# One layer of a hybrid DeltaNet and sliding-window attention encoder: four edits to the order and width of small steps in a fused kernel

## The chip, the cores and the metric

The kernel runs on one core of a Trainium2 chip. The metric is the device time of the program in microseconds (us); less is better. The core's engines are TensorE (PE in the profile, its weight loads PEld), VectorE (DVE), ScalarE (ACT), GpSimd (POOL) and SyncE (SP, which issues DMAs here). Each works through its own list of instructions in order, and they meet only at semaphores.

## The reference

One layer over 2048 positions of width 1024, in fp32:

```python
h = rms_norm(x, norm_w)
z = h @ w_in     # q,k,v of branch A, b_a, a_a (8 columns each), z_a; q,k,v,z of branch B; gates
qkv = silu(causal_depthwise_conv(concat([qa, ka, va]), conv_w))      # 4 taps
beta = sigmoid(b_a);  g = -exp(a_log) * softplus(a_a + dt_bias)
oa = gated_delta_rule(l2(qa), l2(ka), va, g, beta)                   # chunks of 64
# per chunk and head, n_mat strictly lower triangular, 64 x 64:
#   t_mat = I + n_mat; p = n_mat
#   5 times: p = p @ p;  t_mat = t_mat + t_mat @ p
ya = (rms_norm(oa, gdn_norm_w) * silu(z_a)) @ w_o_a
ob = swa_sink_attention(qb, kb, vb, sinks, bias) * silu(z_b)         # window of 2 chunks
m = sigmoid(gate_a) * ya + sigmoid(gate_b) * (ob @ w_o_b)
out = rms_norm(x + m @ w_out, final_norm_w)
```

There are 8 DeltaNet heads with keys and values of 128, and 16 attention heads of 64 on 2 key heads.

## The kernel before

The sequence is cut into 4 blocks (`b`) of 512 positions, each with 4 chunk pairs (`t`, 128 positions). Every large product is a "gemm" of one weight tile of 1024 x 128 (`USES` lists their order): 8 steps over the contraction, each of three matmuls of 128x512 (L1214, L1215, L1216), since an fp32 factor is split into a high and a low part of type fp32r. A block has 3 tiles of prologue (`pro`: beta and decay padded from 16 to 128 columns, then the attention's keys and values), 48 of heads (6 each), 16 gates, 8 + 8 for the branches' output projections (`ya`, `yb`) and 8 for `out`. In block 0 each tile comes fresh: SP loads it, ACT rounds the high part (`high_part`, L485), POOL subtracts the low part (L408), SP stores both to HBM; later blocks load that copy into one of three slots.

Branch A and B of head `h` run in `head`, while the projections of head `h+1` fill the gaps: on PE, ACT and DVE `project` is a generator, and `fill(n)` runs its next n steps. These counts are written by hand, and they set each engine's order.

On DVE the steps of `project` are, for each of q, k and v: one scaling (L923) and three multiply-adds of the convolution (L927), of which the last increments `conv_ready[i]`, then the product with the tanh (L909); and then L909 for za and zb. On ACT they are, in order: copy q, copy k, tanh of q's convolution, copy v, tanh of k's convolution (L575, which waits for `conv_ready[1]`), the three copies of the attention's q, tanh of v's, and two tanhs more.

In `head`, after the decay matrix and k.kT, DVE writes the strictly lower matrix (L970), POOL having given `rk` (a power, L421) for it. PE transposes it (L1400). Five levels follow on PE, each with `square` (p = p @ p, L1331) and `apply` (p @ [p | t], L1347) for the two halves `g` of the chunks, and a sixth `apply`; ACT and DVE copy the results back between them. Then the state goes through the four chunk pairs: PE k.s (L1421), q.s (L1426), DVE r (L1057), PE y (L1431), ACT copies y (L706), PE the state's increment (L1436), DVE the state (L1063) and o (L1067). On ACT this part is written as

```python
state(2)          # o1 copy (L703), y copy (L706)
fill(1)           # tanh of k's convolution
probs_copy(1)
square_o(1)
fill(1)           # three copies of the attention's q
state(3)
```

At the end POOL takes another power (`rqo`), PE transposes o (L1449), and DVE multiplies it into za (L1095) and splits it into `oa_hi` (L1098) and `oa_lo` (L1099), which increments `head_dve_done`.

## Time and profile before

| | |
|---|---|
| median of 3 runs | 2762.26 us (2761.41 to 2763.84) |
| the profiled execution: its own time | 2763.31 us |
| its span in the trace | 2761.2 us, granted TensorE clock 0.999 |
| PE busy | 2722.1 us, 99% of the span |
| DVE, ACT, POOL busy | 1400.4, 981.4, 408.7 us |
| one head in block 1, PE's L1302 to the next head's | 54.85 us (1042.21 to 1097.04) |

How to read it: a row of the timeline gives the start, the time from the first start to the last end, the engine, line and operation, what is written and read, shapes, and how many instructions are merged in it; in brackets is the engine's idle time before it and what ended that. PE's matmuls overlap in the records (one of 128x512 shows 0.39 us, while the next starts 0.23 us after it), so on PE the distance between starts is what counts. An fp32 matmul shows as two records. A "q" after an engine's name is its sequencer, which issues DMAs.

### The profile page before, as it was taken

The numbers are of one execution on the slowest core, as the hardware profiler recorded it, in microseconds if no ns is written. First come the engines' busy times: TensorE is split into PE (matmuls) and PEld (weight loads), VectorE is DVE, ScalarE is ACT, GpSimd is POOL, SyncE is SP. The second block draws the span as 40 slices with busy tenths as digits, with TensorE's granted clock in tenths as the row PEclk, the third lists the DMA queues.
The fourth block names the chain that finished last, engine by engine and source line by source line (L and its number), as shares of the span: only waits on it lengthen the run. The fifth ranks groups of instructions, "written<-read, shape, count | busy, mean of one in ns | idle before, by whom it ended". The sixth has DMA issues, their size and how long they took to land.

```text
span 2761.2 us, 50479 instructions
## 1 busy us (share of the span) xinstructions
PE 2722.1 (99%) x19888; PEld 2305.2 (83%) x19888; DVE 1400.4 (51%) x3529; ACT 981.4 (36%) x3165; POOL 408.7 (15%) x240
## 2 busy tenths in 40 slices
PE   7999999999999999999999999999999999999998
PEld 6888888888888888888888888888888888888887
DVE  5677777323266666622236666661224666665012
ACT  4554555432244444421114444442112444434101
POOL 4333333343210101000000011000000011000000
PEclk9999999999999999999999999999999999999999
DMA  7554445688643233345563333325555333333564
GB/s 259 188 183 157 169 172 185 228 281 295 253 143 127 99 121 125 125 180 209 190 222 120 110 123 124 116 106 203 210 192 209 123 110 125 123 114 108 184 227 168
DMA packets 79577, 463.08 MB, mean 168 GB/s; under 512 B 13296, under 2 KB 17392, under 8 KB 31856
## 3 DMA queue, kind: packets, MB, share of 16 engines
q1 hardware_dynamic: 65808, 430.47, 43.7%
q10 hardware_dynamic: 13536, 29.40, 3.0%
q8 instruction: 160, 2.62, 0.4%
q14 instruction: 73, 0.60, 0.1%
HBM read 356.02 MB, written 103.81 MB: 167 GB/s over the span
## 4 chain that ended last, share of the span: by engine, by line
PE 93%; DVE 3%; DMA 1%; POOL 1%; issue 1%; ACT 0%; ACTq 0%; DVEq 0%; SPq 0%; POOLq 0%
PE bank L1214 23%; PE bank L1216 23%; PE bank L1215 23%; PE bank L1347 5%; PE bank L1331 3%; PE bank L1314 2%; PE bank L1393 1%; PE bank L1431 1%; PE bank L1302 1%; PE bank L1436 1%; PE bank L1385 1%; PE bank L1378 1%; PE bank L1370 1%; PE bank L1439 1%; PE bank L1426 1%; PE bank L1421 1%
## 5 line engine op out<-in xcount | busy, mean ns | idle before, releaser
L1214 PE MATMUL bank<-hT_hi,w_sl 128*128 128x512 f32 x2144 | 885.9, 413 | 0.7 <-ACT hT_hi L516 0.7
L1216 PE MATMUL bank<-hT_hi,w_sl 128*128 128x512 f32 x2144 | 838.9, 391 | 0.0
L1215 PE MATMUL bank<-hT_lo,w_sl 128*128 128x512 f32 x2144 | 836.7, 390 | 0.0
L1216 PEld LDWEIGHTS bank<-hT_hi,w_sl 128*128 128x128 f32 x2144 | 402.4, 188 | 88.1
L1214 PEld LDWEIGHTS bank<-hT_hi,w_sl 128*128 128x128 f32 x2144 | 403.9, 188 | 72.7 <-ACT hT_hi L516 0.9
L1215 PEld LDWEIGHTS bank<-hT_lo,w_sl 128*128 128x128 f32 x2144 | 404.6, 189 | 66.3 <-issue 0.7
L408 POOL TENSOR_TENSOR w_sl<-w_raw,w_sl 128x1024 fp32r<-128x1024 f32 x91 | 222.0, 2444 | 399.4 <-ACT w_sl L485 399.4
L927 DVE SCALAR_TENSOR_TENSOR area<-zraw,stc,area 128x512 f32<-128x512 f32 x288 | 220.3, 765 | 4.2
L1347 PE MATMUL bank<-area 64*64 64x128 f32 (+1 forms) x3072 | 197.9, 245 | 1.1 <-issue 0.6
L822 DVE TENSOR_SCALAR area<-bank 128x128 f32<-128x128 f32 (+1 forms) x320 | 101.4, 317 | 154.8 <-PE bank L1347 114.5
L1063 DVE SCALAR_TENSOR_TENSOR s_cur<-s_cur,scs,bank 128x128 f32<-128x128 f32 x128 | 44.5, 348 | 240.8 <-PE bank L1436 240.8
L1347 PEld LDWEIGHTS bank<-area 64*64 64x64 f32 x3072 | 146.1, 134 | 3.7 <-issue 1.6
L1331 PE MATMUL bank<-area 64*64 64x64 f32 x2560 | 140.0, 222 | 3.5 <-issue 0.5
L427 POOL TENSOR_TENSOR gu<-mk,g_hi 128x512 fp32r<-128x512 f32 x32 | 43.1, 1346 | 635.4 <-DVE r_sb L1057 597.8
L657 ACT ACTIVATE area<-bank 128x128 f32<-128x128 f32 x320 | 88.6, 277 | 110.6 <-PE bank L1331 107.7
L575 ACT ACTIVATE area<-area 128x512 f32<-128x512 f32 x96 | 60.5, 630 | 189.3 <-DVE area L927 189.3
L485 ACT ACTIVATE w_sl<-w_raw 128x1024 fp32r<-128x1024 f32 x91 | 96.2, 1058 | 82.4 <-PE bank L1216 43.9
L1331 PEld LDWEIGHTS bank<-area 64*64 64x64 f32 x2560 | 109.9, 133 | 17.0 <-issue 12.4
L421 POOL TENSOR_TENSOR rqo<-qo,half 128x8 f32<-128x8 f32 x32 | 52.4, 1638 | 436.7 <-DVE qo L1080 436.7
L1214 PE MATMUL bank<-oa_hi,w_sl 128*128 128x512 f32 x256 | 100.5, 393 | 0.0
L1214 PE MATMUL bank<-w_sl,oa_hi 128*128 128x512 f32 x256 | 100.5, 392 | 0.0
L1127 DVE SCALAR_TENSOR_TENSOR area<-area,bank 128x512 f32<-128x512 f32 x28 | 19.3, 688 | 159.6 <-PE bank L1216 159.6
(212 smaller groups left out, 4534.5 us busy)
## 6 DMA issues: line engine op xcount, KB each, us to landing
w_sl<-saved_w SPq DMA_DIRECT2D x273, 1024.0 KB, 4.8
saved_w<-w_sl SPq DMA_DIRECT2D x91, 1024.0 KB, 4.9
w_raw<-in_w_tiles SPq DMA_DIRECT2D x91, 512.0 KB, 5.9
area<-in_x ACTq DMA_DIRECT2D x4, 2048.0 KB, 9.2
area<-in_x ACTq DMA_DIRECT2D x14, 512.0 KB, 7.5
out_y<-area ACTq DMA_DIRECT2D x3, 2048.0 KB, 7.3
bias_sb<-in_bias ACTq DMA_DIRECT2D x32, 128.0 KB, 2.2
out_y<-area ACTq DMA_DIRECT2D x4, 512.0 KB, 2.9
```

The lines of the kernel that those rows point to most:

```text
L408: pool.tensor_tensor(w_sl[:, s, 1, :], w_raw[:, f % 2, :], w_sl[:, s, 0, :].bitcast(F32), ALU.subtract).then_inc(lo_ready, 1)
L485: act.activation(w_sl[:, s, 0, :], w_raw[:, f % 2, :], ACT.Copy).then_inc(hi_ready, 1)
L575: act.activation(ez[i % 2], qkv[:, par, i, :], ACT.Tanh, scale=0.5).then_inc(tanh_z[i], 1)
L657: act.activation(p_sb[l % 2][:, PAIR[g], :], pv(bank[P_BANK[g]])[:, PAIR[g], :], ACT.Copy).then_inc(p_ready[g], 1)
L822: return dve.tensor_scalar(dst, src, 1.0, None, ALU.mult)
L927: ins = dve.scalar_tensor_tensor(acc, zraw[:, i, k:k + TB], stc[:, par, CONV * i + k:CONV * i + k + 1], acc, ALU.mult, ALU.add)
L1214: pe.matmul(dst, a_hi, b_hi, start=first, stop=False)
L1215: pe.matmul(dst, a_hi, b_lo, start=False, stop=False)
L1216: return pe.matmul(dst, a_lo, b_hi, start=False, stop=last)
L1314: ins = pe.matmul(dst[:, t, :], k[:, c], src[:, c], start=True, stop=True)
L1331: ins = pe.matmul(pv(bank[P_BANK[g]])[lo:hi, t, :], ptt[lo:hi, t, 0:CH], p_sb[(l - 1) % 2][lo:hi, t, :], start=True, stop=True)
L1347: ins = pe.matmul(bch(A_BANK[g])[lo:hi, t, c0:c1], p_sb[(l - 1) % 2][lo:hi, t, :], ptt[lo:hi, t, c0:c1], start=True, stop=True)
```

## The change

Four edits.

1. **Beta and decay as 32 resident columns.** The padded weight tile of the prologue goes. Its 16 columns are loaded once, and split by DVE into high and low part side by side (`ba_w`, 32 columns). In each block PE runs 16 matmuls with 32 stationary columns in place of 24 with 128, in an own step `beta_decay_steps`, into bank 7; ACT copies it, PE transposes it, and DVE adds the two halves with one instruction more.
2. **The output's split.** L1098 and L1099 of head h move from its end to head h+1, behind the matrix and its copy (L975) and ahead of the logits; for head 7 they stay at the end.
3. **The second logits' max.** The reduction and the negation move from before r of chunk pair 0 to behind it, in the place of a `fill(1)`, and the `fill(4)` ahead of L1095 becomes `fill(5)`.
4. **Late powers trimmed.** Square 5 computes 32 of 64 columns, apply 5 computes 48 of 64, apply 6 32 of 64; ACT's and DVE's copies shrink with them. Four copies (`settled`) bring the finished part of t to its place, and the four additions of `diagonal` shrink from 64 x 2x64 to 32 x 2x32.

The core of the diff:

```diff
         P_BANK, A_BANK = (5, 7), (6, 2)
+        def first_column(l):
+            return CH if l < LEVELS else CH + 2 ** (l - 1)
         PAIR = (slice(0, 2), slice(2, 4))
...
                 ch = Chain(act, act_pro, b * ACT_PRO)
-                product(n)
-                act.activation(ba_t, bank[bank_of(n)][:, :], ACT.Copy).then_inc(z_read[bank_of(n)], 1)
-                refill(n)
+                act.wait_ge(ba_product, b1)
+                act.activation(ba_t, bank[7][:, :], ACT.Copy).then_inc(ba_copied, 1)
                 yield
...
                 ch.link(act.activation(vb[:, 0:CH], vb[:, TB:TB + CH], ACT.Copy))
-                product(n + 1)
-                act.activation(kb[:, CH:CH + TB], bank[bank_of(n + 1)][:, :], ACT.Copy).then_inc(z_read[bank_of(n + 1)], 1)
-                refill(n + 1)
+                product(n)
+                act.activation(kb[:, CH:CH + TB], bank[bank_of(n)][:, :], ACT.Copy).then_inc(z_read[bank_of(n)], 1)
+                refill(n)
                 yield
...
                 act.activation(pa[:, 3, :, :], pa[:, 1, :, :], ACT.Exp).then_inc(exps, 1)
-                product(n + 2)
-                act.activation(vb[:, CH:CH + TB], bank[bank_of(n + 2)][:, :], ACT.Copy).then_inc(z_read[bank_of(n + 2)], 1)
+                product(n + 1)
+                act.activation(vb[:, CH:CH + TB], bank[bank_of(n + 1)][:, :], ACT.Copy).then_inc(z_read[bank_of(n + 1)], 1)
                 act.wait_ge(sp_in, b1)
                 act.activation(pa[:, 1, :, :], pa[:, 4, :, :], ACT.Ln).then_inc(lns, 1)
-                refill(n + 2)
+                refill(n + 1)
                 yield
...
                     act.wait_ge(p_done[g], n5 + l)
-                    act.activation(p_sb[l % 2][:, PAIR[g], :], pv(bank[P_BANK[g]])[:, PAIR[g], :], ACT.Copy).then_inc(p_ready[g], 1)
+                    width = CH if l < LEVELS else CH - LAST
+                    act.activation(p_sb[l % 2][:, PAIR[g], 0:width], pv(bank[P_BANK[g]])[:, PAIR[g], 0:width], ACT.Copy).then_inc(p_ready[g], 1)
...
             norm_x(0)
+            dve.wait_ge(ba_in, 16)
+            dve.tensor_scalar(ba_w[:, :, 0:2 * H], ba_raw, 1.0, None, ALU.mult).then_inc(dve_init, 1)
+            dve.wait_ge(dve_init, 2)
+            dve.tensor_tensor(ba_w[:, :, 2 * H:4 * H], ba_raw, ba_w[:, :, 0:2 * H].bitcast(F32), ALU.subtract).then_inc(dve_init, 1)
             for k in range(0, KT, 2):
...
                 dve.tensor_copy(ba[:, :, :], bch(6)[:, :, 0:2 * H]).then_inc(ba_read, 1)
-                dve.wait_ge(ba_read, b1)
+                dve.wait_ge(ba_read, 2 * b + 1)
+                dve.tensor_tensor(ba[:, :, :], bch(6)[:, :, 2 * H:4 * H], ba[:, :, :], ALU.add).then_inc(ba_read, 1)
+                dve.wait_ge(ba_read, 2 * b1)
                 y = pa[:, 0, :, :]
...
+            def output_split(b, hh):
+                n1, zat = b * H + hh + 1, za[:, hh % 2, :]
+                dve.wait_ge(ot_read, n1)
+                oah = oa_hi[:, hh, :]
+                dve.tensor_scalar(oah, zat, 1.0, None, ALU.mult).then_inc(oa_high, 1)
+                dve.wait_ge(oa_high, n1)
+                dve.tensor_tensor(oa_lo[:, hh, :], zat, oah.bitcast(F32), ALU.subtract
+                                  ).then_inc(head_dve_done, 1)
             def head(b, hh, fill):
...
                 ins.then_inc(tt0_ready, 1)
+                if hh:
+                    output_split(b, hh - 1)
                 def attention():
...
                             dve.wait_ge(tt_ready[g], (n1 - 1) * (LEVELS - 1) + l - 2)
-                        dve.tensor_tensor(ptt[:, PAIR[g], CH:P], a[:, PAIR[g], CH:P], ptt[:, PAIR[g], CH:P], ALU.add).then_inc(tt_ready[g], 1)
+                        c0 = first_column(l)
+                        dve.tensor_tensor(ptt[:, PAIR[g], c0:P], a[:, PAIR[g], c0:P], ptt[:, PAIR[g], c0:P], ALU.add).then_inc(tt_ready[g], 1)
+                def settled():
+                    for g in range(2):
+                        dve.wait_ge(tt_ready[g], n1 * (LEVELS - 1))
+                        for lo, hi in HALVES:
+                            ins = copy(tt[lo:hi, PAIR[g], lo:hi], ptt[lo:hi, PAIR[g], CH:P])
+                    ch.inc(ins)
                 def diagonal():
+                    ch.sync()
                     for g in range(2):
                         dve.wait_ge(a_done[g], n6 + (LEVELS + 1))
-                        dve.wait_ge(tt_ready[g], n1 * (LEVELS - 1))
                         for lo, hi in HALVES:
-                            ins = dve.tensor_tensor(tt[lo:hi, PAIR[g], lo:hi], bch(A_BANK[g])[lo:hi, PAIR[g], CH:P], ptt[lo:hi, PAIR[g], CH:P], ALU.add)
+                            part = slice(lo, lo + CH - LAST)
+                            ins = dve.tensor_tensor(tt[part, PAIR[g], lo + LAST:hi], bch(A_BANK[g])[part, PAIR[g], CH + LAST:P],
+                                                    ptt[part, PAIR[g], CH + LAST:P], ALU.add)
                     ins.then_inc(diag_ready, 1)
...
                                                  bias_sb[:, par, 1:2, :].to_broadcast([P, NT - 1, P]), ALU.add))
+                def logits_max(g):
                     ch.sync()
...
                 logits(0)
+                logits_max(0)
                 attention()
...
                     level(l, 1)
+                settled()
                 diagonal()
...
                                              ).then_inc(r_ready, 1)
-                    if t != 2:
+                    if t == 0:
+                        logits_max(1)
+                    elif t != 2:
                         fill(1)
...
                 dve.tensor_tensor(o_sb, o_sb, fo[:, :, None].to_broadcast([P, NT, P]), ALU.mult).then_inc(on_ready, 1)
-                fill(4)
+                fill(5)
                 dve.wait_ge(ot_done, n1)
...
                 dve.scalar_tensor_tensor(zat, bank[4][:, :], gnw[:, 0:1], zat, ALU.mult, ALU.mult).then_inc(ot_read, 1)
-                dve.wait_ge(ot_read, n1)
-                oah = oa_hi[:, hh, :]
-                ch.link(dve.tensor_scalar(oah, zat, 1.0, None, ALU.mult))
-                dve.tensor_tensor(oa_lo[:, hh, :], zat, oah.bitcast(F32), ALU.subtract
-                                  ).then_inc(head_dve_done, 1)
                 fill(99)
+                if hh == H - 1:
+                    output_split(b, hh)
                 assert ch.k == DVE_HEAD, ch.k
...
+            def beta_decay_steps(j):
+                pe.wait_ge(bc_ready, j + 1)
+                for k in range(KT):
+                    pe.matmul(bank[7][0:4 * H, :], ba_w[:, k, :], hT_hi[:, k, :], start=k == 0, stop=False)
+                    last = pe.matmul(bank[7][0:4 * H, :], ba_w[:, k, :], hT_lo[:, k, :], start=False, stop=k == KT - 1)
+                    if k == KT - 1:
+                        last.then_inc(ba_product, 1)
+                    yield
             def gemm(n, v_hi, v_lo):
...
                         for lo, hi in HALVES:
-                            ins = pe.matmul(pv(bank[P_BANK[g]])[lo:hi, t, :], ptt[lo:hi, t, 0:CH], p_sb[(l - 1) % 2][lo:hi, t, :], start=True, stop=True)
+                            ins = pe.matmul(pv(bank[P_BANK[g]])[lo:hi, t, 0:width], ptt[lo:hi, t, 0:CH], p_sb[(l - 1) % 2][lo:hi, t, 0:width], start=True, stop=True)
                     ins.then_inc(p_done[g], 1)
...
-                    c0, c1 = (0 if l < LEVELS else CH), (P if l > 1 else CH)
+                    c0, c1 = (0 if l < LEVELS else first_column(l)), (P if l > 1 else CH)
                     if l == 1:
...
                     pe.wait_ge(h_lo, (b + 2) * KT)
+                    for _ in beta_decay_steps(b + 1):
+                        pass
                     gemm(n, hT_hi, hT_lo)
+                    beta_decay(b + 1)
                     gemm(n + 1, hT_hi, hT_lo)
-                    beta_decay(b + 1)
-                    gemm(n + 2, hT_hi, hT_lo)
                 for half_n in range(2):
```

What this does to DVE's order in chunk pairs 1 to 3 of a head's state loop (here the first head; area1 holds the convolutions, area2 scratch, r_sb is r, s_cur the state). Before:

```order
L1030 TENSOR_TENSOR area2<-area2,rden 128x512
L927 SCALAR_TENSOR_TENSOR area1<-zraw,stc,area1 128x512
L1057 SCALAR_TENSOR_TENSOR r_sb<-bank5,negc,area2 128x128
L1063 SCALAR_TENSOR_TENSOR s_cur<-s_cur,scs,bank6 128x128
L1067 TENSOR_TENSOR area2<-bank7,o1_sb 128x128
L909 SCALAR_TENSOR_TENSOR area1<-area2,area1 128x512
L923 TENSOR_SCALAR area1<-zraw,stc 128x512
L1057 SCALAR_TENSOR_TENSOR r_sb<-bank5,negc,area2 128x128
```

And in the changed kernel (its lines 943, 925, 939, 1097, 1105 and 1109 are 927, 909, 923, 1057, 1063 and 1067 of before):

```order
L1068 TENSOR_TENSOR area2<-area2,rden 128x512
L943 SCALAR_TENSOR_TENSOR area1<-zraw,stc,area1 128x512
L1097 SCALAR_TENSOR_TENSOR r_sb<-bank5,negc,area2 128x128
L1105 SCALAR_TENSOR_TENSOR s_cur<-s_cur,scs,bank6 128x128
L1109 TENSOR_TENSOR area2<-bank7,o1_sb 128x128
L943 SCALAR_TENSOR_TENSOR area1<-zraw,stc,area1 128x512
L925 SCALAR_TENSOR_TENSOR area1<-area2,area1 128x512
L1097 SCALAR_TENSOR_TENSOR r_sb<-bank5,negc,area2 128x128
```

The first L927 of the first list is the last of k's three multiply-adds, ahead of r of pair 2. In the second list that last one is the second L943, behind o of pair 2, and k's product with its tanh stands right behind it, ahead of r of pair 3. ACT's list has the same order as before in this place.

On DVE at a head's end and the next one's start, before:

```order
L1095 SCALAR_TENSOR_TENSOR za<-bank4,gnw,za 128x512
L1098 TENSOR_SCALAR oa_hi<-za 128x512
L1099 TENSOR_TENSOR oa_lo<-za,oa_hi 128x512
L909 SCALAR_TENSOR_TENSOR zb<-area2,bank0 128x512
L822 TENSOR_SCALAR s_cur<-s_all 128x128
L954 TENSOR_SCALAR negc<-scs 128x4
L956 TENSOR_SCALAR ssk<-ssq 128x4
```

And now:

```order
L1137 SCALAR_TENSOR_TENSOR za<-bank4,gnw,za 128x512
L925 SCALAR_TENSOR_TENSOR zb<-area2,bank1 128x512
L832 TENSOR_SCALAR s_cur<-s_all 128x128
L979 TENSOR_SCALAR negc<-scs 128x4
L981 TENSOR_SCALAR ssk<-ssq 128x4
```

The two instructions of the split are gone from here, so ssk, on which POOL's power for rk waits, comes two instructions earlier.

On PE, levels 4 to 6 (L1331 square, L1347 apply, L1393 the attention's values) before:

```order
L1347 MATMUL bank<-area 64x128 x4
L1331 MATMUL bank<-area 64x64 x4
L1347 MATMUL bank<-area 64x64 x4
L1331 MATMUL bank<-area 64x64 x4
L1347 MATMUL bank<-area 64x64 x4
L1393 MATMUL bank<-area,vwin 64x64 x8
L1347 MATMUL bank<-area 64x64 x8
```

And now:

```order
L1398 MATMUL bank<-area 64x128 x4
L1382 MATMUL bank<-area 64x32 x4
L1398 MATMUL bank<-area 64x48 x4
L1382 MATMUL bank<-area 64x32 x4
L1398 MATMUL bank<-area 64x48 x4
L1444 MATMUL bank<-area,vwin 64x64 x8
L1398 MATMUL bank<-area 64x32 x8
```

The count of matmuls is the same; five groups are narrower.

## Rows read from the trace of the kernel before

**Rows 1.** The page, part 1: busy us, share of the span, instructions.

```profile
PE 2722.1 (99%) x19888; PEld 2305.2 (83%) x19888; DVE 1400.4 (51%) x3529; ACT 981.4 (36%) x3165; POOL 408.7 (15%) x240
```

**Rows 2.** Timeline of PE, one out tile: start us, us, instruction, count.

```profile
688.88 0.39 PE L1214 MATMUL bank<-w_sl,oa_hi 128*128 128x512 f32 x1
...
694.10 0.40 PE L1216 MATMUL bank<-w_sl,oa_lo 128*128 128x512 f32 x1
```

**Rows 3.** Timeline of PE: matmuls with a 128-column stationary matrix.

```profile
52.86 0.83 PE L1284 MATMUL bank<-sc_all,mk 128*128 128x32 f32 x6 [0.35 <-ACT vwin L557]
...
1096.88 1.04 PE L1302 MATMUL bank<-mk,area 128*128 128x128 f32 x8
```

**Rows 4.** Timeline of PE, block 1: levels 4 and 5.

```profile
1119.05 0.63 PE L1347 MATMUL bank<-area 64*64 64x128 f32 x8
...
1119.74 0.43 PE L1347 MATMUL bank<-area 64*64 64x64 f32 x8
```

**Rows 5.** Timeline of all engines, block 1, around chunks 2 and 3.

```profile
1138.06 0.62 ACT L575 ACTIVATE area<-area 128x512 f32<-128x512 f32 x1
...
1139.58 0.28 DVE L1067 TENSOR_TENSOR area<-bank,o_sb 128x128 f32<-128x128 f32 x1
...
1139.78 0.68 DVE L909 SCALAR_TENSOR_TENSOR area<-area 128x512 f32<-128x512 f32 x1
...
1140.61 0.37 ACT L703 ACTIVATE o_sb<-bank,scs 128x128 f32<-128x128 f32 x1
...
1140.77 0.34 DVE L1057 SCALAR_TENSOR_TENSOR r_sb<-bank,negc,area 128x128 f32<-128x128 f32 x1
...
1142.20 0.28 ACT L706 ACTIVATE y_sb<-bank 128x128 f32<-128x128 f32 x1 [1.23 <-PE bank L1431]
...
1142.70 0.38 PE L1436 MATMUL bank<-y_sb,area 128*128 128x128 f32 x2
...
1147.13 1.53 DVE L927 SCALAR_TENSOR_TENSOR area<-zraw,stc,area 128x512 f32<-128x512 f32 x2
...
1148.76 0.63 ACT L575 ACTIVATE area<-area 128x512 f32<-128x512 f32 x1 [4.58 <-DVE area L927]
```

**Rows 6.** Timeline of all engines, block 0, the same place.

```profile
456.11 0.34 DVE L1057 SCALAR_TENSOR_TENSOR r_sb<-bank,negc,area 128x128 f32<-128x128 f32 x1
...
456.51 0.49 PE L1431 MATMUL bank<-r_sb,area 128*128 128x128 f32 x2 [0.29 <-DVE r_sb L1057]
...
457.21 0.62 ACT L575 ACTIVATE area<-area 128x512 f32<-128x512 f32 x1
...
458.72 0.28 DVE L1067 TENSOR_TENSOR area<-bank,o_sb 128x128 f32<-128x128 f32 x1
...
460.50 0.36 ACT L703 ACTIVATE o_sb<-bank,scs 128x128 f32<-128x128 f32 x1
...
461.87 0.38 PE L1436 MATMUL bank<-y_sb,area 128*128 128x128 f32 x2
```

**Rows 7.** Timeline of all engines, block 0, a head's start.

```profile
470.07 4.89 POOL L408 TENSOR_TENSOR w_sl<-w_raw,w_sl 128x1024 fp32r<-128x1024 f32 x2 [4.61 <-ACT w_sl L485]
...
472.76 2.75 DVE L1099 TENSOR_TENSOR oa_lo<-za,oa_hi 128x512 fp32r<-128x512 f32 x1
...
476.47 1.38 POOL L421 TENSOR_TENSOR rk<-ssk,half 128x4 f32<-128x4 f32 x1 [1.51 <-DVE ssk L956]
...
479.72 0.63 PE L1400 MATMUL bank<-mk,area 128*128 128x128 f32 x4 [0.81 <-DVE area L970]
```

**Rows 8.** Timeline of DVE, block 1, before the logits and behind level 5.

```profile
1106.32 0.29 DVE L1019 TENSOR_TENSOR area<-bank,bias_sb 128x128 f32<-128x128 f32 x1 [2.82 <-PE bank L1370]
...
1121.88 1.20 DVE L1003 TENSOR_TENSOR area<-bank,area 64x128 f32<-64x128 f32 x4 [0.71 <-PE bank L1347]
```

**Rows 9.** Timeline of the first microseconds.

```profile
30.49 0.69 DVE L847 TENSOR_TENSOR hT_lo<-zb,hT_hi 128x512 fp32r<-128x512 f32 x1
...
34.60 0.66 PE L1275 MATMUL bank<-mk,zraw 128*128 128x128 f32 x4
```

More of the change, by code:

```diff
@@ L22 @@
 LEVELS = 5
+LAST = 2 ** LEVELS
 HEAD_TILES = 6
-PRO_TILES = 3
+PRO_TILES = 2
 GATE_TILES = 2 * KT
@@ L446, in _ @@
             pool.wait_ge(const_in, 16 * 4)
-            low(HEAD_TILES)
+            low(HEAD_TILES - 1)
             for b in range(NB):
@@ L1469, in _ @@
             beta_decay(0)
-            gemm(n + 2, hT_hi, hT_lo)
+            gemm(n + 1, hT_hi, hT_lo)
             for i, _ in enumerate(project(0, 0)):
```

39 lines of the change are left out of this document (21 added, 18 removed).

## Prediction, made before the changed kernel was run

> **What bounds the kernel now.** I read the page first: PE is busy 99% of the span [rows 1], at a granted clock of 0.999, that is at its 2.4 GHz level. So time comes or goes in two ways alone: PE's own stream gets shorter or longer, or a wait on PE appears or goes. The timeline of PE gives the prices of the stream, the one of all engines the waits.
>
> The stream: from the first to the last of an out tile's 24 matmuls are 23 steps in 5.22 us, so one of 128x512 costs 0.227 us and a tile 5.45 us [rows 2]. The short fp32 matmuls show two prices. With a stationary matrix of 128 columns, six records that stream 32 columns start 0.11 us apart (0.83 less some 0.28 for the last, over 5 gaps), and eight that stream 128 columns too (1.04 less 0.27, over 7) [rows 3]. With 64 stationary columns, two halves run side by side: 8 records of 128 columns cover 0.63 us, 8 of 64 columns 0.43 us [rows 4]; less one record of 0.27 and 0.22 and the second half's delay of 0.03, over three steps, that is 0.11 and 0.06 us from pair to pair.
>
> The waits: in blocks 1 to 3 PE's rows show hardly any. In block 0 PE waits 0.81 us for DVE's strictly lower matrix [rows 7], in each of 7 heads.
>
> **The change, part by part.** All against the profiled execution's own time, 2763.3 us, which is 1.0 us above the median of the runs.
>
> Third edit, the max and the `fill` counts. Here I expect most. With one `fill(1)` gone from chunk pair 0, each step of the next head's projection falls one place back. The one that matters is k's last multiply-add. It stood ahead of r of pair 2; now it stands behind o of pair 2. ACT's list is unchanged, and ACT is in order: the tanh of k's convolution stands between `state(2)` and `probs_copy(1)`, and it can start only when that multiply-add is done. Before, it started at 1138.06. Now: o of pair 2 starts at 1139.58, and the next DVE instruction 0.20 later; one multiply-add of the pair of 1.53 is some 0.74, and ACT picks up a finished one 0.10 after its end (1147.13 + 1.53, and 1148.76) [rows 5]. 1139.58 + 0.20 + 0.74 + 0.10 = 1140.62. From that tanh to o1 of pair 3 ACT has 1140.61 - 1138.06 = 2.55 us of work without a gap; o1 then starts at 1143.17, the copy of y some 0.27 later, lasts 0.28, and PE starts some 0.06 behind a result that it waits for (r: 456.11 + 0.34, PE at 456.51 [rows 6]). That is 1143.78 for PE's state increment, which started at 1142.70 [rows 5]: 1.08 late. A pair of matmuls that had to wait takes 0.49 in place of 0.38 [rows 5, 6]: 0.1 more. So 1.2 us for a head. Queued behind the waiting tanh are the copy of the probabilities, a square, the three copies of q, o1 and y; on DVE the product with the tanh stands ahead of r of pair 3, so r is late as well (tanh's end 1141.24, product 0.6, r at 1141.95 in place of 1140.77), but by less than y. In 3 blocks with 7 such heads (head 7 has no next head to project): 21 x 1.2 = +25.2.
>
> Block 0 has a fresh tile's rounding of 1.05 us in the same piece of ACT's list: 460.50 - 457.21 = 3.29. So 458.72 + 0.20 + 0.74 + 0.10 + 3.29 + 0.27 + 0.28 + 0.06 = 463.66 against 461.87 [rows 6], 1.8 and 0.1 more: 7 x 1.9 = +13.3.
>
> The max itself wins nothing: r of pair 0 is not late in any head, so bringing it 0.9 us forward shortens no wait. The fifth step ahead of L1095 lengthens DVE's end of a head by 0.74 us, where it idles as long for ACT; I cost it at nothing, and without that cover it is 0.7 us a head.
>
> Second edit, the split. In blocks 1 to 3 it lands in 2.82 us of idle DVE time ahead of the logits [rows 8], and PE did not wait at the head's start: nothing. In block 0 it could take the whole 0.81 us off, 7 x 0.81 = 5.7. But DVE's product there ran 2.75 us [rows 7] while POOL's two low parts filled 470.07 to 474.96, and it ended only 0.55 us behind them; what now comes forward (the state's copy, negc, ssk) is again SBUF work on DVE, in the same stretch, and POOL's power for rk (476.47) is queued behind both low parts anyway. ACT's list also brings them later now, by the 0.7 us above. So the gain lies between 0 and 5.7; I take 0.3 a head, nearer to none: -2.1.
>
> The Trainium skill's page "SBUF — State Buffer", section "SBUF: two separate sides", has a rule for this: VectorE and GpSimd share one pair of ports as an exclusive lock, and a two-port or two-input VectorE instruction blocks fully while GpSimd's holds it. By that rule the gain would be 0 and the sum 2.1 higher; without it 5.7, and the sum 3.6 lower. The 2.75 us row agrees with the rule.
>
> First edit, beta and decay. In blocks 1 to 3, 24 matmuls of 0.227 go and 16 of about the same come; what streams is 512 columns as before, so (24 - 16) x 0.227 = 1.8 each, -5.4. A narrow stationary matrix could be cheaper still; the floor is 512 columns at 2.4 GHz, 0.213, which would give 0.2 more for each block. DVE's addition hides behind the values' gemm (5.45 us). In block 0's prologue the two first gemms ran interleaved with DVE's h. PE's beta transposes started at 34.60, 3.4 us behind the last low part's end at 31.18 [rows 9]; five matmuls must follow it (1.1), and ACT's copy (some 0.6), so at most 1.7 can be won, less DVE's two new instructions ahead of h, which may meet POOL's first low parts. I take -1.0 out of 0 to 1.7.
>
> Fourth edit, the trims. Streaming fewer columns should pay only where streaming is what sets the pace. With 128 stationary columns it does not: 32 and 128 columns cost the same 0.11 [rows 3]. Half as many stationary columns should then have half that floor, 0.055, and the 64-column pairs stand at 0.06 already [rows 4]. So I take 0 for the trims, with 16.0 as the other end (below). On DVE, four small copies come in, in the 0.71 us of idle time ahead of the final additions, which are narrower than their 1.20 now [rows 8]; PE has 1.4 us of `fill(2)` as cover there. Without cover it would be some 0.2 us a head.
>
> The sum: 25.2 + 13.3 - 2.1 - 5.4 - 1.0 = +30.0, so 2793.3 on the profiled execution's scale, and 2792.3 on the median's. Against 2762.3 that is 1.1% slower. A measurement of this kernel can tell about 0.2% from no change, 5.5 us.
>
> **The rivals.**
>
> A. The trims pay. Streaming alone prices a pair at 0.05 us for each 64 columns (0.11 less 0.06). Per head, square 5 saves 32 columns in 8 pairs, apply 5 saves 16 in 8, apply 6 saves 32 in 8: 8 x (0.025 + 0.0125 + 0.025) = 0.5, times 32 is 16.0 us, and 2792.3 - 16.0 = 2776.3. Against it is the equal price in rows 3; for it, that no row has 64 stationary columns with fewer than 64 streamed. The skill's page "TensorE: Matmul & The Clock Gate", section "Back-to-back issue gap", has the gap of an isolated matmul as the columns over the clock and 2.5 ns, which would be this rival; its next section, on LDWEIGHTS, has a load's time as the stationary columns over 1.2 (107 ns for 128, 53 for 64), which the 0.11 us of rows 3 agrees with.
>
> B. On the other side: the tanh is in time, and PE never sees the shift. ACT idled 1.23 us before y of pair 3 [rows 5], so the point that decides is whether k's last multiply-add ends more than 1.2 us before my 1140.52, that is before 1139.3, when o of pair 2 has not yet begun. If r or the increment of pair 2 came that much earlier on PE, the whole of 38.5 falls away: 2762.3 - 2.1 - 5.4 - 1.0 = 2753.8, faster. PE's stream ahead of it is full, and nothing in it changes, so I give it little.
>
> C. Block 0 does worse: later low parts on POOL meet DVE's copies and small instructions of the state loop's end, and DVE's end of a head, longer by 0.7, reaches PE. One further wait of 1.2 us in each of 7 heads makes 2792.3 + 8.4 = 2800.7.
>
> D. The wait is hidden in part, and block 0's waits go fully, with the trims paying: 2792.3 - 16.0 - 3.6 = 2772.7 before any of the tanh's wait is hidden; a third of that wait hidden (12.8) would end near no change, 2759.9.
>
> **How the numbers follow.** My forecast 0.76, A 0.07, B 0.05, C 0.09, D 0.03. The time is that of the first, 2792. Range: its own terms may be off by 0.2 us in each of 28 heads (5.6) and by the bounds of the split (-3.6, +2.1), the startup and the trims' small part; C's 2800.7 is taken in with some room above it, and A's 2776 stands just inside the lower end: 2775 to 2803. What is left out is B and D. Faster by over 0.2%: 0.05 from B and 0.01 of D; within: 0.02 of D and 0.01 of the rest; slower: 0.91.
>
> **What would show it.** Right: ACT's tanh of k, for heads 0 to 6, starts some 0.1 us behind a multiply-add that follows o of pair 2, with an idle time of over 2 us before it that DVE ends; PE's state increment of pair 3 waits for ACT's y in 28 heads; a head in block 1 takes 56.0 us in place of 54.85; the narrow matmuls of levels 5 and 6 start as far apart as the wide ones did; PE's 0.81 us wait in block 0 is still there, smaller. Wrong: no wait ahead of the increment of pair 3, or narrow pairs that start 0.03 us apart (A), or heads of block 0 that grew by over 3 us (C).

## The result and the profile after

The changed kernel takes 2785.96 us, the median of 4 runs (2784.97 to 2786.51), against 2762.59 of the kernel before (2761.41 to 2763.84). The ratio is 1.0084, 95% interval 1.0072 to 1.0097: 23.4 us slower, where 29.7 were forecast (2792, range 2775 to 2803).

The page of the changed kernel, part 1 (busy us, share of the span of 2784.4, instructions), answers to [rows 1]:

```profile
PE 2729.4 (98%) x19856; PEld 2290.8 (82%) x19856; DVE 1433.1 (51%) x3663; ACT 974.2 (35%) x3164; POOL 387.0 (14%) x239
```

PE has 32 records fewer and 7.3 us more of busy time, in a span that is 23.2 us longer. The busy share (98%) doesn't tell where the 23 us went. The distance from one head's start to the next does, taken at the first transpose of its k (L1302 before, L1351 now):

| | before | changed |
|---|---|---|
| first head starts at | 75.9 us | 75.6 us |
| block 0, heads 0 to 7 (7 distances) | 395.0 | 404.8 |
| blocks 1, 2, 3 | 384.4, 385.2, 384.7 | 390.7, 391.0, 391.6 |
| head 7 to the next block's head 0 | 296.5, 295.5, 295.5 | 294.4, 293.8, 293.8 |
| from the last head's start | 248.6 | 248.7 |

A typical head of block 1 takes 55.81 us in place of 54.85 (the two starts given beside that number in the table of the kernel before are 54.83 apart). The sum of the table's differences is 9.8 + 19.0 - 5.5 - 0.3 + 0.1 = 23.1. What PE waited for, in the view of waits (us in total, times, longest):

```profile
PE bank L1482 <- DVE r_sb L1097: 12.0, 35, 0.4
PE bank L1487 <- ACT y_sb L716: 7.1, 7, 1.0
PE bank L1451 <- DVE area L993: 2.7, 7, 0.4
```

Before, the first of them stood at 2.1 us in 7 times, the second did not stand there, and the third stood at 6.1 us in 8. The timeline of block 1 around chunk pairs 2 and 3 answers to [rows 5]:

```profile
1152.44 0.28 DVE L1109 TENSOR_TENSOR area<-bank,o_sb 128x128 f32<-128x128 f32 x1
...
1152.64 0.74 DVE L943 SCALAR_TENSOR_TENSOR area<-zraw,stc,area 128x512 f32<-128x512 f32 x1
...
1153.48 0.63 ACT L584 ACTIVATE area<-area 128x512 f32<-128x512 f32 x1 [2.45 <-DVE area L943]
...
1154.15 0.69 DVE L925 SCALAR_TENSOR_TENSOR area<-area 128x512 f32<-128x512 f32 x1 [0.76 <-ACT area L584]
...
1154.76 0.34 DVE L1097 SCALAR_TENSOR_TENSOR r_sb<-bank,negc,area 128x128 f32<-128x128 f32 x1
...
1155.16 0.49 PE L1482 MATMUL bank<-r_sb,area 128*128 128x128 f32 x2 [0.35 <-DVE r_sb L1097]
...
1155.84 0.36 ACT L713 ACTIVATE o_sb<-bank,scs 128x128 f32<-128x128 f32 x1
...
1156.09 0.28 ACT L716 ACTIVATE y_sb<-bank 128x128 f32<-128x128 f32 x1
...
1156.42 0.49 PE L1487 MATMUL bank<-y_sb,area 128*128 128x128 f32 x2
```

Read it from the first row, o of pair 2. The multiply-add L943 stands behind it. ACT's tanh (L584) has idled 2.45 us and starts 1.04 us behind o; before, it had started 1.52 ahead of it. DVE's product (L925) waits 0.76 for the tanh, so r of pair 3 is at +2.32 in place of +1.19, and y waits 0.35 for it. ACT comes to o1 at +3.40 and copies y at +3.65. PE's increment L1487 is at +3.98; it had been at +3.12. It starts 0.05 us behind the end of ACT's copy of y in all 28 heads; in blocks 1 to 3 PE has idled only 0.07 us by then, too little for the view of waits, which lists block 0's 7 alone. In block 0, against [rows 6], the same piece has a rounding of a fresh tile in ACT's list as well:

```profile
466.42 0.28 DVE L1109 TENSOR_TENSOR area<-bank,o_sb 128x128 f32<-128x128 f32 x1
...
467.46 0.63 ACT L584 ACTIVATE area<-area 128x512 f32<-128x512 f32 x1 [2.45 <-DVE area L943]
...
470.76 0.36 ACT L713 ACTIVATE o_sb<-bank,scs 128x128 f32<-128x128 f32 x1
...
471.34 0.49 PE L1487 MATMUL bank<-y_sb,area 128*128 128x128 f32 x2 [1.02 <-ACT y_sb L716]
```

The increment is 4.92 behind o in place of 3.15. At a head's start in block 0, against [rows 7]:

```profile
480.78 4.72 POOL L417 TENSOR_TENSOR w_sl<-w_raw,w_sl 128x1024 fp32r<-128x1024 f32 x2 [5.40 <-ACT w_sl L495]
...
481.24 0.68 DVE L925 SCALAR_TENSOR_TENSOR zb<-area,bank 128x512 f32<-128x512 f32 x1
...
481.84 1.39 DVE L832 TENSOR_SCALAR s_cur<-s_all 128x128 f32<-128x128 f32 x1
...
483.15 2.38 DVE L979 TENSOR_SCALAR negc<-scs 128x4 f32<-128x4 f32 x1
...
485.44 0.15 DVE L981 TENSOR_SCALAR ssk<-ssq 128x4 f32<-128x4 f32 x1
...
485.68 1.38 POOL L430 TENSOR_TENSOR rk<-ssk,half 128x4 f32<-128x4 f32 x1 [0.18 <-DVE ssk L981]
...
488.90 0.63 PE L1451 MATMUL bank<-mk,area 128*128 128x128 f32 x4 [0.37 <-DVE area L993]
```

PE's wait for the strictly lower matrix is 0.37 now, from 0.81. While POOL's two low parts run (480.78 to 485.50) the state's copy and `negc` are stretched: 128x4 in 2.38 us. ssk comes the moment they end, and POOL's power for rk has idled 0.18 us where it had idled 1.51. The levels, against [rows 4], on PE:

```profile
1132.33 0.42 PE L1382 MATMUL bank<-area 64*64 64x32 f32 x8
1132.56 0.44 PE L1398 MATMUL bank<-area 64*64 64x48 f32 x8
...
1134.22 0.66 PE L1398 MATMUL bank<-area 64*64 64x32 f32 x16
1134.80 0.50 PE L1253 MATMUL bank<-hT_hi,w_sl 128*128 128x512 f32 x1
```

Eight records with 32 streamed columns cover 0.42 us and with 48 columns 0.44, where eight with 64 covered 0.43.

### The profile page after: what moved, and what is told of

Same layout as the page of the kernel before. It is cut to its first block, busy times and chain, and to the rows that moved or that the text cites. A ratio compares the mean times of both kernels' runs of the same rounds, so it can differ in the third digit from the quotient of the medians.

```text
span 2784.4 us, 50472 instructions
## 1 busy us (share of the span) xinstructions
PE 2729.4 (98%) x19856; PEld 2290.8 (82%) x19856; DVE 1433.1 (51%) x3663; ACT 974.2 (35%) x3164; POOL 387.0 (14%) x239
## 3 DMA queue, kind: packets, MB, share of 16 engines
q8 instruction: 160, 2.62, 0.4%
## 4 chain that ended last, share of the span: by engine, by line
PE 88%; DVE 5%; ACT 3%; issue 1%; POOL 1%; DMA 1%; ACTq 0%; DVEq 0%; POOLq 0%
PE bank L1253 22%; PE bank L1255 21%; PE bank L1254 21%; PE bank L1398 5%; PE bank L1382 3%; PE bank L1363 2%; DVE area L943 1%; PE bank L1487 1%; PE bank L1444 1%; PE bank L1351 1%; PE bank L1436 1%; PE bank L1429 1%; PE bank L1482 1%; PE bank L1421 1%; PE bank L1477 1%
## 5 line engine op out<-in xcount | busy, mean ns | idle before, releaser
L1253 PE MATMUL bank<-hT_hi,w_sl 128*128 128x512 f32 x2112 | 873.7, 414 | 0.0
L1255 PE MATMUL bank<-hT_hi,w_sl 128*128 128x512 f32 x2112 | 826.6, 391 | 0.0
L1254 PE MATMUL bank<-hT_lo,w_sl 128*128 128x512 f32 x2112 | 825.2, 391 | 0.0
L1255 PEld LDWEIGHTS bank<-hT_hi,w_sl 128*128 128x128 f32 x2112 | 396.6, 188 | 86.8
L1253 PEld LDWEIGHTS bank<-hT_hi,w_sl 128*128 128x128 f32 x2112 | 398.1, 188 | 71.4 <-issue 1.0
L1254 PEld LDWEIGHTS bank<-hT_lo,w_sl 128*128 128x128 f32 x2112 | 398.7, 189 | 65.1 <-issue 0.7
L943 DVE SCALAR_TENSOR_TENSOR area<-zraw,stc,area 128x512 f32<-128x512 f32 x288 | 220.4, 765 | 4.2
L1398 PE MATMUL bank<-area 64*64 64x128 f32 (+3 forms) x3072 | 197.4, 245 | 0.9 <-issue 0.9
L584 ACT ACTIVATE area<-area 128x512 f32<-128x512 f32 x96 | 60.7, 632 | 280.3 <-DVE area L943 280.3
L1382 PE MATMUL bank<-area 64*64 64x64 f32 (+1 forms) x2560 | 138.4, 221 | 3.5 <-issue 0.5
L436 POOL TENSOR_TENSOR gu<-mk,g_hi 128x512 fp32r<-128x512 f32 x32 | 34.0, 1064 | 650.6 <-DVE r_sb L1097 613.2
L667 ACT ACTIVATE area<-bank 128x128 f32<-128x128 f32 (+1 forms) x320 | 85.2, 266 | 111.2 <-PE bank L1382 108.3
```

The lines of the kernel that those rows point to most:

```text
L584: act.activation(ez[i % 2], qkv[:, par, i, :], ACT.Tanh, scale=0.5).then_inc(tanh_z[i], 1)
L667: act.activation(p_sb[l % 2][:, PAIR[g], 0:width], pv(bank[P_BANK[g]])[:, PAIR[g], 0:width], ACT.Copy).then_inc(p_ready[g], 1)
L943: ins = dve.scalar_tensor_tensor(acc, zraw[:, i, k:k + TB], stc[:, par, CONV * i + k:CONV * i + k + 1], acc, ALU.mult, ALU.add)
L1253: pe.matmul(dst, a_hi, b_hi, start=first, stop=False)
L1254: pe.matmul(dst, a_hi, b_lo, start=False, stop=False)
L1255: return pe.matmul(dst, a_lo, b_hi, start=False, stop=last)
```

## The experiments

All times are medians, beside runs of the kernel before on the same chip; ratios are to those, with 95% intervals.

| kernel | us | ratio |
|---|---|---|
| third edit alone | 2811.2 | 1.0171 (1.0157 to 1.0185) |
| fourth edit alone | 2761.6 | 0.9998 (0.9989 to 1.0007) |
| second edit alone | 2754.7 | 0.9970 (0.9959 to 0.9982) |
| first edit alone | 2755.5 | 0.9973 (0.9964 to 0.9983) |
| changed, old fill counts | 2747.3 | 0.9942 (0.9929 to 0.9954) |
| changed, tanh later on ACT | 2772.8 | 1.0035 (1.0022 to 1.0047) |
| max behind r alone | 2762.7 | 0.9999 (0.9990 to 1.0008) |
| mended order | 2740.9 | 0.9919 (0.9906 to 0.9933) |
| changed, second edit undone | 2801.1 | 1.0136 (1.0120 to 1.0152) |
| changed, 32 stationary columns | 2775.3 | 1.0044 (1.0031 to 1.0057) |
| mended order, narrow matrices | 2736.0 | 0.9905 (0.9889 to 0.9922) |

### Each edit alone

**The third edit alone**, on the kernel before:

```diff
                 logits(0)
+                logits_max(0)
...
-                    if t != 2:
+                    if t == 0:
+                        logits_max(1)
+                    elif t != 2:
                         fill(1)
...
-                fill(4)
+                fill(5)
```

> The kernel before with the third edit alone (second logits' max behind the first r, one fill less in chunk pair 0, fill(5) at the end). Theory of the waiting tanh: all of the loss is here. The traces show a head's pitch grown by 0.90 us in blocks 1 to 3 (19.0 over 21 heads) and by 1.41 us in block 0, there with the split's gain of some 0.5 in it: 19.0 + 7 x 1.9 = 32.3 us, so some 2795. In its trace the tanh of k starts 1.04 us behind the start of o of pair 2 and the increment of pair 3 starts 3.98 behind it in block 1, 4.92 in block 0. Rival, the levels' new copies or the split's new place cost the time: this kernel stays within 5 us of 2762.

It took 2811.2, 48.9 us more than before, not 32. Its tanh and its increment of pair 3 stand where the theory put them (+1.04; +3.97 in block 1, +4.92 in block 0), and blocks 1 to 3 grew by 18.4 us. But block 0 grew by 27.3 in place of 13. PE's waits:

```profile
PE bank L1405 <- DVE area L970: 14.0, 8, 1.9
...
PE bank L1441 <- ACT y_sb L706: 7.1, 7, 1.0
```

L1405 is the transpose of the strictly lower matrix. It waits up to 1.9 us in each of the heads 1 to 7 of block 0, where the changed kernel waits 0.4. So this edit has a second cost, most of which the second edit hides; the run without the split takes it up. Part of it comes and goes with the clock: one of its four executions took 2804.7 us at a mean granted clock of 0.998, the others 2810.4 to 2812.6 at 0.995 or 0.996.

**The fourth edit alone:**

> The kernel before with the fourth edit alone (narrower square 5, apply 5 and 6, four settled copies). Theory: a small matmul's pace does not fall with its streamed columns once they are no more than its 64 stationary ones, and the settled copies are hidden: 2762 to 2763. Rival A, streaming sets the pace: 16.0 us less, 2746. Rival, the settled copies reach PE at 0.2 us a head: 2769.

2761.6, no change. The settled copies are hidden, and the trims give nothing.

**The second edit alone:**

> The kernel before with the second edit alone (oa_hi and oa_lo written in the next head). Theory: nothing in blocks 1 to 3, and in block 0 about half of the wait for the strictly lower matrix goes, as between the two traces (7.36 us of start-to-start excess over 7 heads before, 3.84 after): 3.5 us less, 2758.8. Rival, two-engine contention on DVE's product keeps the wait as it is: 2762.3. Rival, the whole 0.81 goes when ACT's list is not late: 5.7 less, 2756.6.

2754.7, 7.5 us less, which is more than any of the three expectations. Block 0's seven distances fell by 7.1 us, and the wait ahead of the strictly lower matrix's transpose is gone in all heads but the first.

**The first edit alone:**

> The kernel before with the first edit alone (beta and decay as 32 resident columns, 16 matmuls in place of 24). Theory: 8 matmuls of 0.227 us fewer in each of three blocks, 5.4, and 0.3 in block 0's prologue, where the first head starts 0.3 us sooner: 5.7 less, 2756.6. Rival, DVE's added instructions and POOL's list, one low part shorter, hold PE elsewhere in block 0: 2762. Rival, a 32-column stationary matrix streams faster than a 128-column one: below 2755.

2755.5, 6.7 us less. Each transition between blocks is 1.7 us shorter (294.8, 293.8, 293.8), and 8 matmuls of 0.227 make 1.8. The first head starts no more than 0.1 us sooner. The rest, 1.5 us, is within what the runs can tell, and one trace of each kernel can't place it: with the old prologue the first head starts at 75.8 to 77.6 us in five traces, with the new one at 75.5 to 76.3 in eight.

### The third edit, taken apart

**The changed kernel with the old counts:**

```diff
                     if t == 0:
                         logits_max(1)
-                    elif t != 2:
+                    if t != 2:
                         fill(1)
...
-                fill(5)
+                fill(4)
```

> The changed kernel with the old fill counts again (a fill(1) behind the max in chunk pair 0, fill(4) at the end); the max stays behind the first r, the other three edits stay. Theory of the waiting tanh: the pitches of blocks 1 to 3 go back to 54.85 us and the increment of pair 3 to 3.13 us behind o of pair 2; with the three other edits alone at -0.6, -7.5 and -6.7 us the sum is 2747.4. Rival, it is the max's new place that delays the state's first pairs: the time stays over 2775.

2747.3, on the sum of the other three edits alone. The increment of pair 3 is 3.12 us behind o of pair 2 again. So the counts cost 38.7 us in the changed kernel: 20.9 in blocks 1 to 3 and 17.8 in block 0 (387.0 against 404.8).

Block 0's share has a second part, at a head's start. First the changed kernel, ahead of the rows shown for that place, and then this one, where the head starts at 463.32 (480.46 in the changed kernel):

```profile
476.22 2.32 DVE L943 SCALAR_TENSOR_TENSOR area<-zraw,stc,area 128x512 f32<-128x512 f32 x3
...
478.63 0.63 ACT L584 ACTIVATE area<-area 128x512 f32<-128x512 f32 x1 [5.71 <-DVE area L943]
```

```profile
458.76 1.53 DVE L943 SCALAR_TENSOR_TENSOR area<-zraw,stc,area 128x512 f32<-128x512 f32 x2
...
460.38 0.63 ACT L584 ACTIVATE area<-area 128x512 f32<-128x512 f32 x1 [4.58 <-DVE area L943]
...
462.53 4.71 POOL L417 TENSOR_TENSOR w_sl<-w_raw,w_sl 128x1024 fp32r<-128x1024 f32 x2 [4.61 <-ACT w_sl L495]
...
467.42 1.38 POOL L430 TENSOR_TENSOR rk<-ssk,half 128x4 f32<-128x4 f32 x1 [0.18 <-DVE ssk L981]
...
471.21 0.60 PE L1451 MATMUL bank<-mk,area 128*128 128x128 f32 x4
```

The step that was taken out of chunk pair 0 comes back here as a third multiply-add of v, ahead of v's tanh. ACT's tanh starts 1.83 us ahead of the head's start in place of 2.94, and behind it in ACT's list stand the roundings that POOL's two low parts wait for. These start 0.32 us behind the head's start, not 0.79 ahead of it: 1.1 us later. ssk and POOL's power come right behind them in both kernels, so the strictly lower matrix is later too, and PE waits for it.

**The tanh moved back on ACT**, so that less is queued behind it:

```diff
                 state(2)
-                fill(1)
                 probs_copy(1)
                 square_o(1)
                 fill(1)
+                fill(1)
                 state(3)
```

> The changed kernel with ACT's fill(1) of k's tanh moved two steps back, behind the copy of the probabilities and the square of o; DVE's order stays that of the changed kernel. Theory, the loss is what is queued behind the waiting tanh: those two pieces (some 0.5 and 0.5 us) now run ahead of it, so the increment of pair 3 starts some 3.5 us behind o of pair 2 in place of 3.98 in blocks 1 to 3 and 4.4 in place of 4.92 in block 0; r of pair 3 stays late, since DVE's product with the tanh stands ahead of it. 28 x 0.47 = 13 less than 2786, so 2773. Rival, the increment is late because r and y are, and ACT's queue does not count: 2786 as before.

2772.8. In its timeline, block 1, the increment is 3.74 behind o of pair 2 (982.87 less 979.13), a quarter of a us later than expected, since y itself is late for r:

```profile
979.13 0.28 DVE L1109 TENSOR_TENSOR area<-bank,o_sb 128x128 f32<-128x128 f32 x1
...
980.17 0.63 ACT L584 ACTIVATE area<-area 128x512 f32<-128x512 f32 x1 [1.40 <-DVE area L943]
...
981.75 0.36 ACT L713 ACTIVATE o_sb<-bank,scs 128x128 f32<-128x128 f32 x1
...
982.37 0.28 ACT L716 ACTIVATE y_sb<-bank 128x128 f32<-128x128 f32 x1 [0.26 <-PE bank L1482]
...
982.87 0.38 PE L1487 MATMUL bank<-y_sb,area 128*128 128x128 f32 x2
```

The tanh starts at the same +1.04, but ACT reaches o1 at +2.62 and then waits 0.26 for y. In block 0 the increment is at +4.14, better than the 4.4 expected. So the 13 us came as forecast, but by some luck: 7.2 in blocks 1 to 3, where less than expected was won, and 5.6 in block 0, where more was. Both parts of the theory stand. What is queued behind the tanh on ACT makes these 13 us. Of the 25.5 us left against the old counts, y of pair 3, late by 0.5 for r and by 0.1 in its pair, makes 21 x 0.6 = 13 in blocks 1 to 3. In block 0 ACT doesn't idle ahead of y, so its own list is still what is late: the increment by 1.0 and its pair by 0.1, 7 x 1.1 = 8; the wait at the head's start is the rest, 3.8.

**The max alone**, with all counts as before:

> The kernel before with only the second logits' max behind the first r, all fill counts as they were. Prediction's view: r of pair 0 is not late, so 2762 (no change). Rival, r comes 0.9 us sooner and that shortens something on PE: each 0.1 us a head would be 3.2 us less.

2762.7: the new place of the max is worth nothing and costs nothing.

### The split as a cover

**The changed kernel with the second edit undone:**

```diff
                 ins.then_inc(tt0_ready, 1)
-                if hh:
-                    output_split(b, hh - 1)
...
+                oah = oa_hi[:, hh, :]
+                ch.link(dve.tensor_scalar(oah, zat, 1.0, None, ALU.mult))
+                dve.tensor_tensor(oa_lo[:, hh, :], zat, oah.bitcast(F32), ALU.subtract
+                                  ).then_inc(head_dve_done, 1)
                 fill(99)
-                if hh == H - 1:
-                    output_split(b, hh)
```

> The changed kernel with the second edit undone (oa_hi and oa_lo written at the head's own end again). If the edits add up, it is the split's own 7.5 us slower than the changed kernel's 2786: 2793.5. Theory of the lost cover: the fifth fill step ahead of the product with za is hidden in block 0 only because the split has left that place; without it block 0 waits some 2.1 us for the strictly lower matrix in each head and TensorE's granted clock falls behind that wait, as in the third edit alone: 2811.2 less the first and fourth edit's 6.7 and 0.6, some 2804.

2801.1, 15.1 us more than the changed kernel and close to the lost cover's 2804. The timeline at a head's start in block 0:

```profile
432.91 4.91 POOL L417 TENSOR_TENSOR w_sl<-w_raw,w_sl 128x1024 fp32r<-128x1024 f32 x2 [5.39 <-ACT w_sl L495]
...
433.50 2.06 DVE L1129 TENSOR_SCALAR oa_hi<-za 128x512 fp32r<-128x512 f32 x1
...
435.59 2.77 DVE L1130 TENSOR_TENSOR oa_lo<-za,oa_hi 128x512 fp32r<-128x512 f32 x1
...
439.09 0.16 DVE L972 TENSOR_SCALAR ssk<-ssq 128x4 f32<-128x4 f32 x1
...
439.32 1.38 POOL L430 TENSOR_TENSOR rk<-ssk,half 128x4 f32<-128x4 f32 x1 [1.51 <-DVE ssk L972]
...
442.55 0.63 PE L1443 MATMUL bank<-mk,area 128*128 128x128 f32 x4 [1.93 <-DVE area L984]
```

The two instructions of the split (L1129, L1130) run beside POOL's two low parts and take 2.06 and 2.77 us; in the changed kernel, away from them, they take 0.43 and 0.69 (432.00 and 432.46). POOL's low parts end at 437.82, its power for rk starts 1.50 us later for want of ssk, and PE waits 1.93. Then the clock. The view of windows for this kernel (busy time and records of PE, PEld, DVE, ACT, POOL; granted clock; DMA share; GB/s):

```profile
442.00:443.00 1.00, 0.45 (x4) 0.48 (x5) 0.95 (x4) 0.99 (x5) 0.00 (x0) 1.00 1.04 434
443.00:444.00 1.00, 1.00 (x8) 1.00 (x7) 0.29 (x1) 0.96 (x3) 0.00 (x0) 0.62 0.92 377
444.00:445.00 1.00, 1.00 (x6) 0.90 (x5) 0.26 (x2) 0.97 (x5) 0.00 (x0) 0.50 0.63 218
445.00:446.00 1.00, 1.00 (x4) 0.81 (x3) 0.97 (x3) 0.55 (x3) 0.00 (x0) 0.50 0.46 114
446.00:447.00 1.00, 1.00 (x4) 0.76 (x4) 0.96 (x5) 0.92 (x2) 0.00 (x0) 0.67 0.06 20
447.00:448.00 1.00, 1.00 (x6) 0.82 (x5) 0.96 (x5) 1.00 (x4) 0.29 (x1) 1.00 0.00 0
```

The granted clock stays at 1.00 (2.4 GHz) through the wait, falls to 0.50 (1.2 GHz) here 0.7 us after PE took up work again, and comes back 3.4 us later. The matmuls of 128x512 start 0.427 us apart there in place of 0.227. The 18 records behind the first transpose take 4.34 us, against 2.75 in the changed kernel. This happened behind 3 of the 7 waits here, and behind 5 of 7 in the third edit alone, from 0.04 to 1.4 us after PE had resumed; 26 records on, the loss is 1.6 us each time. In the other cases a wait as long left the clock at 1.00. The waits themselves are 10.6 us longer than in the changed kernel, and with 3 x 1.6 = 4.8 that makes 15.4, against the 15.1 us between the medians. In the third edit alone the clock's part is 5 x 1.6 = 8 us of the profiled execution.

### What sets a small matmul's pace

**The changed kernel with 32 stationary columns** in square 5 and apply 5 and 6:

```diff
-    ins = pe.matmul(pv(bank[P_BANK[g]])[lo:hi, t, 0:width], ptt[lo:hi, t, 0:CH], ...)
+    rows = CH if l < LEVELS else CH - LAST
+    ins = pe.matmul(pv(bank[P_BANK[g]])[lo:lo + rows, t, 0:width], ptt[lo:hi, t, 0:rows], ...)
...
-    ins = pe.matmul(bch(A_BANK[g])[lo:hi, t, c0:c1], p_sb[(l - 1) % 2][lo:hi, t, :], ...)
+    rows = CH if l < LEVELS else CH - LAST
+    ins = pe.matmul(bch(A_BANK[g])[lo:lo + rows, t, c0:c1], p_sb[(l - 1) % 2][lo:hi, t, 0:rows], ...)
```

> The changed kernel with the stationary matrices of square 5, apply 5 and apply 6 cut from 64 to 32 columns; half of the rows of these three products are left out, so the output is not the reference's. They are 48 records a head, 0.029 to 0.032 us from start to start with 64 stationary columns, whether 64, 48 or 32 columns stream. Theory, the stationary matrix's columns set the pace there: 0.015 a record, 0.7 us a head and up to 23 us, less what the waits between the levels take back. Rival, a floor for each matmul whatever its size: the starts stay 0.030 apart and the time 2786. Rival, the streamed columns set it: no change either, and then the fourth edit alone would have saved 16 us, which it did not.

2775.3, 10.7 us less than the changed kernel. On PE in block 1:

```profile
1128.44 0.31 PE L1383 MATMUL bank<-area 64*32 64x32 f32 x8
1128.59 0.34 PE L1400 MATMUL bank<-area 64*32 64x48 f32 x8
...
1130.09 0.44 PE L1400 MATMUL bank<-area 64*32 64x32 f32 x16
```

Eight records of 64x32 cover 0.31 us in place of 0.42, and sixteen 0.44 in place of 0.66. Mean distances between starts, over all heads:

| stationary x streamed | us from start to start |
|---|---|
| 64 x 64, square / apply 1 | 0.031 / 0.026 |
| 64 x 32, square / apply 6 | 0.029 / 0.030 |
| 64 x 48, apply 5 | 0.032 |
| 32 x 32, square / apply 6 | 0.018 / 0.017 |
| 32 x 48, apply 5 | 0.021 |

With 64 stationary columns the distance is 0.026 to 0.032 us and doesn't fall with the streamed columns; half the stationary columns bring it to 0.017 or 0.018. The stationary columns set the pace, not the streamed ones, as long as no more stream than are stationary.

### A version that beats both

**The mended order:**

```diff
                     if t == 0:
                         logits_max(1)
-                    elif t != 2:
-                        fill(1)
+                    fill(1)
...
                         quotient(1)
-                        fill(1)
...
-                fill(5)
+                fill(4)
```

> As the changed kernel with the old counts, and in addition k's last multiply-add moved from ahead of r of pair 2 to just behind it, still ahead of o of pair 2. In both kernels the y pair of chunk pair 2 starts some 0.05 us late for r and its second matmul 0.1 later, 0.16 us in each of 28 heads. Theory: r of pair 2 comes 0.66 us sooner, the tanh is still in time (the multiply-add ends some 0.6 us before ACT comes to the tanh): 4.4 us less than the kernel with the old counts, so 2743. Rival, the tanh is late again: 2747 or more.

2740.9, 0.8% faster than before. The increment stands at +3.14. Against the old counts, block 0 gained 3.3 us and blocks 1 to 3 some 0.9 each. It was expected to gain the same in every head; in block 0 y of pair 2 had waited 0.3 us for r, not 0.05.

**The mended order with narrow matrices:**

```diff
-    ins = pe.matmul(pv(bank[P_BANK[g]])[lo:hi, t, 0:width], ptt[lo:hi, t, 0:CH], ...)
+    first = lo if l < LEVELS else lo + LAST
+    ins = pe.matmul(pv(bank[P_BANK[g]])[first:hi, t, 0:width], ptt[lo:hi, t, first - lo:CH], ...)
...
+    # apply 6 alone
+    ins = pe.matmul(bch(A_BANK[g])[lo:lo + LAST, t, c0:c1], p_sb[(l - 1) % 2][lo + LAST:hi, t, 0:LAST],
+                    ptt[lo + LAST:hi, t, c0:c1], start=True, stop=True)
```

> The mended order of the kernel above (old counts, k's last multiply-add behind r of pair 2), with narrower stationary matrices where the product's other half is zero anyway: square 5 computes rows 32 to 63 alone (32 stationary columns), and apply 6 rows 0 to 31 from positions 32 to 63 alone (32 stationary columns, 32 rows). Nothing is left out. By the pitches measured with 32 stationary columns (0.018 in place of 0.029 us for square 5, 0.017 in place of 0.030 for apply 6), 16 x 0.011 + 16 x 0.013 = 0.38 us a head, 12 us, less the waits between levels 5 and 6: in the run with 32 stationary columns 0.33 of some 0.55 us a head was left. So 0.23 to 0.38 a head, 2729 to 2734 against the mended order's 2740.9. Rival, with only 32 rows, or with the copies now the bound between levels, nothing is left: 2741.

2736.0: 4.9 us less than the mended order, and less than the 7 to 12 expected. The starts are 0.018 us apart in both groups, as expected, but of 12 us some 5 reached the end. The traces of the two kernels show which part (medians over the 32 heads). From apply 6 to the gemm behind it PE is 0.215 us faster, which is all that was hoped for there. Square 5 gives nothing: its first group starts 0.125 us later behind apply 4 than the wide one did, though ACT's and DVE's copies that it waits for end when they did, and from there to the attention's values only 0.05 is won. Together that is 0.14 us a head, 4.4 us in 32 heads. The same 0.125 us stands in the kernel with 32 stationary columns above. What holds the first narrow group back is open; the profile shows nothing that it waits for.

## Why the prediction was right

**The late tanh** is shown. Its start was forecast at 1140.62 with o at 1139.58, which is +1.04, and +1.04 it is in 21 heads of 28 (block 3's heads have +1.07 to +1.09). The sum of the third edit was 38.5 us, and putting the counts back gave 38.7. That agreement is partly luck. In blocks 1 to 3 the forecast was 25.2 and the runs gave 20.9: I took ACT's work from tanh to o1 as 2.55 us "without a gap", but before the change o1 stood 0.04 us behind the end of q.s on PE (1140.57), so 0.2 of it was a wait that now falls away. The increment came at +3.98, not +4.20. In block 0 the increment's delay was right (+4.94 forecast, +4.92 measured, 13.3 us), but the block lost 17.8.

**The fifth fill step** was costed at nothing, with 0.7 us a head as its price without cover. That failed in block 0. With the old counts and the split moved, PE does not wait at the head's start at all; in the changed kernel it waits there seven times, 3.8 us from start to start. That is most of the 4.5 missing. The sum did name the way, that ACT's list brings POOL's low parts later, but gave it 0.7 us and no price; it is 1.1 us. In blocks 1 to 3 there are no low parts, and PE doesn't wait.

**The split** was forecast at 2.1 us out of 0 to 5.7. This is the step that failed. Alone it gives 7.5, and in the changed kernel it holds off 15.1. I argued that POOL's power for rk is queued behind both low parts anyway. But its own row said that POOL had idled 1.51 us ahead of it, waiting for DVE's ssk [rows 7]. So DVE was the later of the two, and whatever left its list there came off PE's wait, until rk stood 0.18 behind the low parts. The upper bound was wrong as well: it took PE's idle time of 0.81 as all that can be won, while from start to start a head lost 1.0 (each first matmul's delay counted by starts, less the usual 0.23). The port rule of the Trainium skill that I weighed ("SBUF — State Buffer", section "SBUF: two separate sides") holds in these rows: beside POOL's low parts a DVE instruction of 128x4 takes 2.38 us in place of 0.16. But from it I worked out a gain of 0, and the rule says only who is stretched. What is stretched is now short work that has to end no sooner than the low parts do.

**Beta and decay** were forecast at 5.4 and 1.0. The three blocks gave 1.7 us each, 5.1. The start gave 0.3 in the changed kernel and 0.1 alone: of the 1.0 taken for it these two pairs of traces show nearly nothing, but the first head's start varies by more than that between traces of kernels with the same prologue, so this term stays open.

**The trims** give nothing, as taken, and for the reason given: 32 and 64 streamed columns cost the same 0.03 us a record, and half the stationary columns cost 0.017. I had taken a formula of the Trainium skill's page "TensorE: Matmul & The Clock Gate", section "Back-to-back issue gap", for the rival in which they pay. That was half a reading: the formula is the page's for an isolated matmul, and the table below it has one figure, some 60 cycles, for all of 1 to 64 columns, by which they would not. The records agree with the table in that 32, 48 and 64 columns cost the same.

**Of the signs**, those named for being right all came: the tanh's start and its idle time, the increment behind ACT's y in 28 heads, 55.8 us for a head of block 1 where 56.0 were named, narrow matmuls as far apart as wide ones, and a smaller wait in block 0.

**Of the rivals**, A is excluded by the fourth edit alone, and B by the tanh's +1.04. C's mechanism, DVE's longer end of a head reaching PE in block 0, is there, at 0.55 us a head and not 1.2, since the split's move took most of it away. Without the split it would have been worse than C. The forecast is 6.3 us too high. Its terms were off by +4.3 (blocks 1 to 3), -4.5 (block 0), +5.4 (the split; 7.5 for 2.1), +0.3 (beta and start together, 6.7 for 6.4) and +0.6 (trims), which is 6.1. The rest is the spread of the medians. So the time came out as near as it did partly because the third edit's two misses, of over 4 us each, cancel; the miss that is left is the split's.
